# Half norms followed by three output tiles side by side, with spreads, row sums and a weight split in other places

## What is computed

```python
for i in range(DEPTH):                      # 2 layers; mixer 0 = Fourier, mixer 1 = Conformer convolution
    m = split((silu(c) @ w_mod[i] + b_mod[i]), 9)          # shift, scale, gate, three times
    h = h + 0.5 * m[2] * swiglu(modulate(rms_norm(h), m[0], m[1]), w_ff_in[i, 0], w_ff_out[i, 0])
    a = modulate(rms_norm(h), m[3], m[4])
    h = h + m[5] * mixer(a)
    h = h + 0.5 * m[8] * swiglu(modulate(rms_norm(h), m[6], m[7]), w_ff_in[i, 1], w_ff_out[i, 1])

def swiglu(h, w_in, w_out):
    g, u = split(h @ w_in, 2)
    return (silu(g) * u) @ w_out
```

## Time and profile before

| | |
|---|---|
| median of 3 runs | 1887.16 us (1886.59 to 1888.53) |
| profiled execution | 1890.15 us, its span 1888.3 us |
| PE busy | 1805.4 us, 96% of the span |
| DVE busy | 1200.4 us, 64% |
| ACT busy | 619.5 us, 33% |
| POOL busy | 161.8 us, 9% |
| mean granted clock of PE | 0.978 of full |

### The profile page before, as it was taken

How to read it: one execution, slowest core, us unless ns; L and a number is a source line. 1 busy time by engine, 2 the same in 40 slices (tenths; PEclk the granted TensorE clock), 3 DMA queues, 4 the chain that set the end, 5 groups by cost and what they waited for, 6 DMA issues and landing times.

```text
span 1888.3 us, 21852 instructions
## 1 busy us (share of the span) xinstructions
PE 1805.4 (96%) x8540; PEld 1484.4 (79%) x8540; DVE 1200.4 (64%) x1546; ACT 619.5 (33%) x795; POOL 161.8 (9%) x145
## 2 busy tenths in 40 slices
PE   5899999999999999999999999999995999999998
PEld 2688888888888888888878888888662788888887
DVE  5877667677486666767876764455888454444454
ACT  2532222234332222222422222225775342222221
POOL 0000000010200000000100000004882200000000
PEclk8999999998999999999999999999997899999999
DMA  8744535340345363543463523221210332322201
GB/s 291 275 174 140 194 111 214 120 141 17 127 153 189 112 220 113 179 154 112 157 222 112 191 98 110 91 68 45 89 45 1 101 118 72 127 74 97 103 22 68
DMA packets 160399, 238.14 MB, mean 126 GB/s; under 512 B 3805, under 2 KB 110509, under 8 KB 160204
## 3 DMA queue, kind: packets, MB, share of 16 engines
q1 hardware_dynamic: 160016, 236.99, 35.9%
q10 hardware_dynamic: 316, 0.23, 0.0%
HBM read 235.11 MB, written 2.10 MB: 126 GB/s over the span
## 4 chain that ended last, share of the span: by engine, by line
PE 79%; DVE 11%; POOL 3%; ACT 3%; issue 2%; DMA 1%; SPq 0%; POOLq 0%; DVEq 0%; ACTq 0%
PE bank L1573 14%; PE bank L1580 14%; PE bank L1575 14%; PE bank L1466 10%; PE bank L1468 10%; PE bank L1467 10%; DVE bank L1419 3%; POOL tmp_c L603 2%; DVE mod_acc L967 2%; DVE w_lo L944 2%; PE bank L1547 1%; DMA raw_pair<-in_w_mod 1%; PE bank L1540 1%; PE bank L1542 1%; POOL sq_sum L568 1%
## 5 line engine op out<-in xcount | busy, mean ns | idle before, releaser
L1573 PE MATMUL bank<-a_hi,w_hi 128*128 128x512 f32 x1408 | 552.8, 393 | 4.7 <-ACT a_hi L651 4.7
L1575 PE MATMUL bank<-a_hi,w_lo 128*128 128x512 f32 x1408 | 549.8, 390 | 0.0
L1580 PE MATMUL bank<-a_lo,w_hi 128*128 128x512 f32 x1408 | 435.5, 391 | 1.4 <-DVE a_lo L1039 1.4
L1573 PEld LDWEIGHTS bank<-a_hi,w_hi 128*128 128x128 f32 x1408 | 265.6, 189 | 61.7 <-issue 6.3
L1155 DVE SCALAR_TENSOR_TENSOR h<-bank,half_gate,h 128x512 f32<-128x512 f32 x320 | 233.6, 746 | 122.6 <-PE bank L1468 121.8
L1580 PEld LDWEIGHTS bank<-a_lo,w_hi 128*128 128x128 f32 x1408 | 265.2, 189 | 57.7 <-DVE a_lo L1039 2.4
L1575 PEld LDWEIGHTS bank<-a_hi,w_lo 128*128 128x128 f32 x1408 | 265.6, 189 | 56.5 <-issue 1.4
L1466 PE MATMUL bank<-p_hi,w_hi 128*128 128x512 f32 (+1 forms) x768 | 287.5, 374 | 6.6 <-DVE h L1162 3.8
L1467 PE MATMUL bank<-p_hi,w_lo 128*128 128x512 f32 (+1 forms) x768 | 286.0, 372 | 0.0
L1468 PE MATMUL bank<-p_lo,w_hi 128*128 128x512 f32 (+1 forms) x768 | 286.0, 372 | 0.0
L944 DVE TENSOR_TENSOR w_lo<-raw_pair,w_hi 128x2048 fp32r<-128x2048 f32 x106 | 245.1, 2313 | 63.1 <-ACT w_hi L761 47.9
(11 more groups left out here) (166 smaller groups left out, 1841.0 us busy)
## 6 DMA issues: line engine op xcount, KB each, us to landing
raw_pair<-in_w_ff_in SPq DMA_DIRECT2D x88, 1024.0 KB, 7.1
raw_mod<-in_w_mod SPq DMA_DIRECT2D x66, 1024.0 KB, 8.1
raw_down<-in_w_ff_out SPq DMA_DIRECT2D x44, 1024.0 KB, 8.6
raw_pair<-in_conv_w_in SPq DMA_DIRECT2D x8, 1024.0 KB, 7.1
raw_pair<-in_w_mod SPq DMA_DIRECT2D x6, 1024.0 KB, 14.5
raw_pair<-in_fnet_w_out SPq DMA_DIRECT2D x4, 1024.0 KB, 6.4
raw_pair<-in_conv_w_out SPq DMA_DIRECT2D x4, 1024.0 KB, 6.3
raw_mod<-in_x SPq DMA_DIRECT2D x4, 512.0 KB, 5.3
```

The costliest lines, as they stand in the source:

```text
L1573: pe.matmul(ps[banks + s][:], tile_hi, a_hi[:, k], start=k == 0, stop=False, skip_group_check=True)
L1575: pe.matmul(ps[banks + s][:], tile_lo, a_hi[:, k], start=False, stop=False, skip_group_check=True)
L1580: ins = pe.matmul(ps[banks + s][:], w_hi[b][:, s * KD + k], a_lo[:, k], start=False, stop=k == KD - 1, skip_group_check=True)
```

## The change

- `first_two` works on three output tiles at once in the first half (both tiles of chunk 0 and the first of chunk 1), k by k; the sums of the second half stay behind k = 2 (`SUM_AT`), the spread goes behind k = 7, and the fourth tile follows. In the second half all four tiles are done side by side for k = 0 and 1, then chunk 0 and chunk 1 for the other six k.
- ACT's root of the second half goes from behind a_hi of k = 7 to behind k = 5, DVE's reciprocal and diagonal from behind a_lo of k = 7 to behind a_lo of k = 5 (n = 2, 3, 4, 6).
- `ff_norm` splits the weight tile in two pieces of 128x1024, behind the half updates 3 and 6 (n = 1, 3, 4).
- `project` spreads the first half behind the fourth k of e = 9, no longer ahead of e = 9 (n = 2, 6).
- In the first step of f = 0, 1, 2 the late unit is summed behind k = 1 of the second up chunk, and for f = 0 and 1 its rows are transposed behind k = 4, no longer ahead of the chunk.

The number and the sizes of matmuls stay as they are; DVE has three instructions more.

```diff
+    SUM_AT = 2
...
@@ ACT ff_norm and project_norm
                     for k in range(4, KD):
                         half_hi(n, 0, k, layer, v)
-                    half_std(n, 1)
+                        if k == 5:
+                            half_std(n, 1)
...
@@ DVE
+            def pair_lo_part(unit, pair, j, part):
+
+                b, use = unit
+                rows = slice(KD * part, KD * (part + 1))
+                dve.wait_ge(s_w_hi[b], use + 1)
+                ins = dve.tensor_tensor(w_lo[b][:, rows], raw_pair[pair % 2][:, rows, j, :],
+                                        w_hi[b][:, rows].bitcast(F32), ALU.subtract)
+                if part == 1:
+                    ins.then_inc(s_w[b], 1)
...
@@ DVE ff_norm
-                for d in range(4):
+                for d in range(KD):
                     flush_half(f, 0, d)
-                next_lo_unit()
-                for d in range(4, KD):
-                    flush_half(f, 0, d)
+                    if d == 3:
+                        next_lo_unit(0)
+                    if d == 6:
+                        next_lo_unit(1)
                 mod_columns(call)
...
@@ DVE ff_norm and project
                         half_normed(n, 0, k, layer, v)
                         half_lo(n, 0, k - 1, layer, v)
+                        if k == 6:
+                            half_rstd(n, 1)
                     half_lo(n, 0, KD - 1, layer, v)
-                    half_rstd(n, 1)
                     half_chunks(n, 1, range(KD), layer, v)
...
@@ PE
+            def half_product(b, s, bank, k, hs, lo):
+
+                if lo:
+                    return pe.matmul(bank[:, hs], w_hi[b][:, s * KD + k], a_lo[:, k, hs], start=False,
+                                     stop=k == KD - 1, skip_group_check=True)
+                pe.matmul(bank[:, hs], w_hi[b][:, s * KD + k], a_hi[:, k, hs], start=k == 0, stop=False,
+                          skip_group_check=True)
+                return pe.matmul(bank[:, hs], w_lo[b][:, s * KD + k], a_hi[:, k, hs], start=False, stop=False,
+                                 skip_group_check=True)
...
+                tiles = [(units[ch][0], s, ps[2 * ch + s]) for ch in range(2) for s in range(2)]
+                for hf in range(2):
+                    hs = HALF[hf]
+                    if hf == 0:
+                        for k in range(KD):
+                            pe.wait_ge(s_half_hi[0], KD * r + k + 1)
+                            for b, s, bank in tiles[:3]:
+                                half_product(b, s, bank, k, hs, False)
+                            pe.wait_ge(s_half_a[0], KD * r + k + 1)
+                            for b, s, bank in tiles[:3]:
+                                half_product(b, s, bank, k, hs, True)
+                            if k == SUM_AT:
+                                half_sums(n, 1)
                         half_spread(n, 1)
...
+                        b, s, bank = tiles[3]
+                        for k in range(KD):
+                            half_product(b, s, bank, k, hs, False)
+                            half_product(b, s, bank, k, hs, True)
+                        continue
+                    for k in range(2):
+                        pe.wait_ge(s_half_a[1], KD * r + k + 1)
+                        for b, s, bank in tiles:
+                            half_product(b, s, bank, k, hs, False)
+                        for b, s, bank in tiles:
+                            half_product(b, s, bank, k, hs, True)
+                    for ch in range(2):
+                        for k in range(2, KD):
+                            if ch == 0:
+                                pe.wait_ge(s_half_a[1], KD * r + k + 1)
+                            for b, s, bank in tiles[2 * ch:2 * ch + 2]:
+                                half_product(b, s, bank, k, hs, False)
+                            for b, s, bank in tiles[2 * ch:2 * ch + 2]:
+                                ins = half_product(b, s, bank, k, hs, True)
+                        ins.then_inc(done, 1)
...
@@ PE step
                     up(f, i, 0, False)
-                    if late_unit:
-
+
+                    def late_sum():
                         pe.wait_ge(s_mod_row, u0 - 1)
                         mod_sum(u0 - 1)
+
+                    among = []
+                    if late_unit:
+                        among = [(1, late_sum)]
                         if f < 2:
-                            mod_transpose(1 + 2 * f)
-                    up(f, i, 1, False)
+                            among.append((4, lambda: mod_transpose(1 + 2 * f)))
+                    up(f, i, 1, False, among)
...
@@ PE project
+                        if k == KD - 1:
+                            ins.then_inc(s_take, 1)
                         if e == 8 and k == 3:
                             half_sums(n, 0)
-                    ins.then_inc(s_take, 1)
-                    if e == 8:
-                        half_spread(n, 0)
+                        if e == 9 and k == 3:
+                            half_spread(n, 0)
```

56 lines of the change are left out of this document (19 added, 37 removed).

## The result

| | before | changed |
|---|---|---|
| median of 20 runs | 1888.3 us | 1892.7 us |
| ratio, with its 95% interval | 1 | 1.0024 (1.0017 to 1.0031) |
| profiled execution | 1890.15 us, span 1888.3 | 1892.88 us, span 1891.0 |
| mean granted clock | 0.978 | 0.979 |

The kernel became slower by 4.4 us, 0.24% by the ratio. The forecast was +2.5 us (1889.7 us, range 1884.5 to 1895.0), so the range holds the time and the sign is right. "Slower by over 0.2%" had only the second largest chance (0.28), "within 0.2%" had 0.64.

A forecast was written before the change was run, and what follows sets the result against it. DVE's longer chains behind the half norms were taken to bound, despite PE busy 96%. Chains +1.0 us (4.4 - 0.6 - 0.1 + 0.25 - 1.0 - 1.9) plus clock +1.5 on 1887.16 gave 1889.7 us, range 1884.5 to 1895.0.

The forecast's parts named there:

- Part 1: First feed-forward, late sum and transposes inside the second chunk: DVE's chain starts later, fourth down tile at 111.5, +4.4 us.
- Part 2: Project, three tiles and second feed-forward: second spread later, modulation sum's chain 1.4 us earlier, fourth down tile 582.8, -0.6 us.
- clock term: Half clock behind new pauses, 0 to 1.7 us for each of three phases: +1.5 us with the chains, bounds 0 and +6.8.
- Part 3: Norms with split w_lo -0.1 us, third phase's fourth down tile +0.25 us, convolution's sigmoid 1.0 us earlier.
- Part 4: Last feed-forward: no waits left in the k loop, w_lo complete earlier, PE goes on at 1540.05, -1.9 us.
- The base: Whole kernel: the +2.5 us were put on the median before, 1887.16 us.
- the Fourier part: Norm before Fourier: splitting w_lo puts half_sums 0.1 us earlier, -0.1 us.
- A: The clock decides: 3.4 us at half clock behind each of four long pauses, +7.8, up to 1895 us; chance 0.26.
- B: PE sets the pace and DVE isn't late, so the pauses go: -23.7 us, 1863.5 us; chance 0.06.
- C: Norms: POOL isn't caught by the w_lo pieces, 3 x 1.1 us less, 1886.4 us; chance 0.10.
- D: The change doesn't do what it says, instructions stand as before; no size or separate chance given.

The follow-up runs named there:

- second profile of before: The kernel before, unchanged, run once more for another profile: 1888.98 us, one run.
- late sum back: Changed kernel with the late sum and the transposes back in front of the second up chunk: 1887.4 us, ratio 0.9990.
- the run of the pieces: Kernel before with only the weight split of the three norms in two pieces: 1889.61 us, ratio 1.0004.
- the spread alone: Kernel before with only the first half's spread behind the fourth k of e = 9 in the two projections: 1885.46 us, ratio 0.9981.
- PE's and DVE's new order: Kernel before, late sum and transposes moved; DVE's late row update behind four accumulations, own row update behind the first chunk's product: 1879.05 us, ratio 0.9950.

## Why the prediction was right, and where it was not

**Part 1, +4.4 us.** Right in mechanism and size. Transposes: 95.0 worked out, 95.84 measured, of which 0.5 is a later start of the whole phase in this execution and 0.2 that the first pair of tiles ends at 87.9 and not at 87.7. From the transposes to the fourth down tile 16.5 us worked out, 112.35 - 95.84 = 16.51 measured, and 586.72 - 570.21 = 16.51 in the second phase. The wait ahead of the sum was 3.73 (3.9 worked out), the last one 1.85 and not 3.6: half clock from 104.0 to 107.4 slowed PE just ahead of a wait, where it costs nothing.

**Part 2, -0.6 us.** Measured: +0.9 against the first profile of before, from e=8 on (+2.44 to +3.31), +0.8 against the second. The steps held up to the sum: DVE's second half starts 0.75 us later (0.5 worked out), the sum behind the two chunks comes 1.3 us earlier (1.4), and PE waits 2.10 us for it (2.3). The step that failed was "the second pair starts when its w_lo is done". DVE's w_lo, the pair's first matmul and its sum:

```profile
559.36 2.29 DVE L947 TENSOR_TENSOR w_lo<-raw_pair,w_hi 128x2048 fp32r<-128x2048 f32 x1 [1.11 <-ACT w_hi L764]
562.81 0.39 PE L1606 MATMUL bank<-a_hi,w_hi 128*128 128x512 f32 x1
565.53 0.40 PE L1489 MATMUL bank<-mod_acc_hi,ones_r 128*36 128x512 f32 x1
```

That w_lo was done at 561.65, and the pair started without a wait at 562.81. PE had been at half clock from 551.16 to 554.57 in the pair ahead of it, which costs 1.7 us, with 0.5 us of slack. The clock term had such a loss among its bounds ("the pause behind the two chunks slows the pair that follows"), but the sum of this part had none.

**Part 3.** Norms: -0.1 each worked out; half_sums of norms 3 and 4 came 0.26 and 0.27 us earlier against the end of the phase ahead. Third phase: PE's sum +0.4 against half_sums (the forecast was 0.25 to 0.35), the fourth down tile +0.4 in all. Convolution: -1.0 stated for the sigmoid (the two dates of the working, 925.66 and 924.83, give -0.8), -0.1 measured (1309.06 against 1305.36 and 3.84 us at the end of the phase ahead). The timeline of ACT:

```profile
1307.18 1.28 ACT L887 ACT_TABLE_LOAD   x1
1309.06 0.69 ACT L887 ACTIVATE tmp_a<-bank,vecs 128x512 f32<-128x512 f32 x1 [0.60 <-PE bank L1551]
```

ACT's wait of 3.47 us for PE has shrunk to 0.60. Half clock from 1285.0 to 1288.4 in the k loop took about 0.6 us of the gain: without it (late sum back) the sigmoid still waits only 0.59 us, and it comes 0.7 us earlier (1303.46, with -1.21 at the end of the phase ahead). That half clock lies where it came with the weight pieces in 12 of 14 norms; the prediction weighed the pieces by POOL's additions alone. What I had as a harmless remark, that DVE's and ACT's work ahead of the sigmoid "still ends at about 1304", is the second bound, 0.6 us in front of it.

**Part 4, -1.9 us.** Measured -1.4 (+4.05 to +2.64). The waits of 1.91 and 0.38 us at the spreads went as forecast, but the second spread came 0.4 us later than worked out (at 1529.09, 0.64 us ahead of the second row below), and w_lo 0.6 us earlier and not 1.1:

```profile
1517.58 0.71 PE L1544 MATMUL bank<-tmp_b,ones 128*128 128x128 f32 x4 [0.48 <-DVE tmp_b L1076]
...
1529.73 0.87 DVE L1091 SCALAR_TENSOR_TENSOR tmp_b<-h,mod,bank 128x256 f32<-128x256 f32 x2 [3.48 <-PE bank L1544]
...
1542.24 2.29 DVE L947 TENSOR_TENSOR w_lo<-raw_pair,w_hi 128x2048 fp32r<-128x2048 f32 x1 [1.12 <-ACT w_hi L764]
```

The term was mis-sized by 0.5 us: the three-tile loop took 11.5 us from the first spread to the second, 0.4 more than the count of matmuls times 0.12 us gives.

**Clock, +1.5 us.** Half clock in sum: 81.9 and 75.1 us in the two profiles of before, 78.5 in the changed kernel. Against the second this is 3.4 us more, which is 1.7 us of time where PE is the bound; against the first it is 3.4 us less. So the size is right by luck. Four of the new pauses had half clock at or behind them (from 104.0, 551.2, 578.5 and 967.6 on), and what that cost depended on the wait behind it: nothing at 104.0, 1.2 us at 551.2.

**The base.** The forecast was put on the median of three runs (1887.16). The median of 20 was 1888.3, and that is 1.1 us of the 3.0 us by which 1892.7 lies above 1889.7.

**The sum.** Against the second profile of before the first phase is +4.6, where the prediction had +4.4. From the end of e=8 on the stretches add up to +0.1 (+0.8, +0.5, -0.05, +0.2, -1.4), where it had -3.3 for the chains and +1.5 for the clock. The Fourier part gave -1.0, where it had -0.1. So part 1 carries the sign and most of the size and was right for its reason; that the traces' sum is no further off than 1.2 us (3.7 for 2.5) owes something to luck: behind e=8 the forecast was 1.9 us too low, in the Fourier part 0.9 too high.

**Rivals.** A (the clock decides, up to 1895) is not what made it slower: taking part 1 out brings the time back, and half clock in sum was no longer than in the first profile of before. Its premise was true all the same, half clock at four of the long pauses, only not its price of 1.7 us each. B (PE sets the pace, 1863.5) falls with the rows of the first phase. C falls with the run of the pieces. D is excluded by the rows.

What stays open: why the changed kernel's +5.2 us of the first phase shrank to +2.4 at e=8 (2.8 us), where the other profiles gave back 1.1 to 1.8, and those with 13.7 us at half clock 0.2. The half clock of the Fourier part explains the difference to the latter, not that to the second profile of before, which had 6.8 us of it as well. And the spread alone on top of PE's and DVE's new order, with two tiles side by side and the whole weight tile, looks like the best combination (the spread alone was worth 0.19%, the three tiles nothing, and the pieces brought half clock); it wasn't tried.
